# Four PSUM banks for the transposed expert rows, and 16-bit integer lookups in the expert choice

## What is computed

```
q = (ht @ w_query).reshape(T, 8, 2, 128)
s = einsum('thpd,hpnd->thpn', q, sub_keys)          # 8 heads, 2 halves, 128 keys
top_s, top_i = top_k(s, 16)
cand_s = top_s[:, :, 0, :, None] + top_s[:, :, 1, None, :]     # 16 x 16 sums a head
cand_i = top_i[:, :, 0, :, None] * 128 + top_i[:, :, 1, None, :]
fin_s, pos = top_k(cand_s, 16)
fin_i = take_along_axis(cand_i, pos)                # 128 experts a token
gate = softmax(fin_s)
out = sum over the 128: gate * gelu(expert_u[fin_i] . x) * expert_v[fin_i]
```

## Time and profile before

| | us |
|---|---|
| median of 3 runs (3353.91 to 3363.41) | 3357.28 |
| the profiled execution's own time | 3359.51 |
| its span in the trace | 3357.8 |
| busy: TensorE matmul / weight load | 3265.7 / 2872.9 |
| busy: VectorE / ScalarE / GpSimd | 2549.1 / 900.3 / 801.7 |
| `peer_topk`, 887.9 to 1511.5 | 623.6 |
| `peer_gates`, 1511.5 to 2267.2 | 755.7 |
| `peer_down`, 2267.2 to the end | 1090.6 |

### The profile page before, as it was taken

The page is one execution under the profiler, slowest core; times in us unless marked ns, Lnnn a source line. Parts: engine busy times, 40 slices in busy tenths (PEclk is TensorE's granted clock), DMA queues, the critical chain, the costliest instruction groups (busy, mean ns, idle before and its releaser), DMA issues. The chain is left out here.

```text
span 3357.8 us, 46048 instructions
## 1 busy us (share of the span) xinstructions
PE 3265.7 (97%) x17796; PEld 2872.9 (86%) x17796; DVE 2549.1 (76%) x5349; ACT 900.3 (27%) x1310; POOL 801.7 (24%) x625
## 2 busy tenths in 40 slices
PE   8999989899999999999999999999999999999998
PEld 7867755499999999999999999997888888888887
DVE  6611244322499999999989898876999999999996
ACT  4210301111122222224444444432222222222222
POOL 0000000000001100104333333342444444444440
PEclk9999989899999999999999999999999999999999
DMA  3010021311144444448889788889898898988883
GB/s 99 14 40 27 13 88 63 119 57 38 46 133 145 144 141 141 134 137 291 304 308 325 279 324 308 308 320 359 312 318 306 314 314 314 312 318 314 316 309 135
DMA packets 332962, 695.58 MB, mean 207 GB/s; under 512 B 34332, under 2 KB 194936, under 8 KB 326584
## 3 DMA queue, kind: packets, MB, share of 16 engines
q1 hardware_dynamic: 248600, 386.28, 33.0%
q0 software_dynamic: 84144, 306.35, 26.7%
HBM read 580.10 MB, written 110.64 MB: 206 GB/s over the span
## 5 line engine op out<-in xcount | busy, mean ns | idle before, releaser
L1782 ACT ACTIVATE up_a<-up_pa 128x384 f32<-128x384 f32 x256 | 126.0, 492 | 830.8 <-PE up_pa L1767 820.9
L1806 POOL DMA_INDIRECT lead<-in_peer_v_dram,idx x174 | 259.6, 1492 | 352.9 <-DVE acc_s L1825 326.7
L2478 DVE TENSOR_TENSOR acc<-pd_po,acc 128x512 f32<-128x512 f32 x384 | 264.6, 689 | 93.3 <-PE pd_po L2537 90.7
L1806 POOL DMA_INDIRECT gr_row<-in_peer_u_dram,idx x192 | 229.9, 1197 | 368.2 <-DVE raw L1815 341.3
L1815 DVE CUSTOM_DVE_ANT_0 gr_row<-gr_row,xs 128x1024 f32<-128x1024 f32 x192 | 232.1, 1223 | 2.1 <-DMA gr_row<-in_peer_u_dram,idx 2.0
L1806 POOL DMA_INDIRECT dr_row<-in_peer_v_dram,idx x114 | 171.1, 1501 | 215.1 <-DVE acc_s L1825 211.7
L1825 DVE SCALAR_TENSOR_TENSOR acc_s<-lead,gate,acc_s 128x1024 f32<-128x1024 f32 x174 | 222.3, 1278 | 0.0
L2264 DVE TENSOR_SCALAR pg_hot_i<-pg_iota,sel_t 128x128 f32<-128x128 f32 x768 | 214.2, 359 | 0.0
L511 PE MATMUL fr_a<-pj_w,h_t 128*128 128x256 f32 (+1 forms) x864 | 200.3, 394 | 0.9 <-PEq L186 0.9
L2299 PE MATMUL pg_pw<-pg_hot_i,pg_hot_j 128*128 128x128 f32 x1536 | 200.5, 276 | 0.1
L511 PEld LDWEIGHTS fr_a<-pj_w,h_t 128*128 128x128 f32 (+1 forms) x864 | 171.0, 227 | 29.7 <-issue 8.4
(11 more groups left out here) (469 smaller groups left out, 7899.0 us busy)
## 6 DMA issues: line engine op xcount, KB each, us to landing
lead<-in_peer_u_dram SPq DMA_DIRECT2D x128, 512.0 KB, 4.9
room<-in_peer_v_dram SPq DMA_DIRECT2D x128, 512.0 KB, 4.5
act_d<-up_a SPq DMA_DIRECT2D x256, 192.0 KB, 3.5
room<-w_d SPq DMA_DIRECT2D x64, 768.0 KB, 6.6
room<-act_d SPq DMA_DIRECT2D x64, 768.0 KB, 9.2
w_d<-room SPq DMA_DIRECT2D x24, 1024.0 KB, 10.6
w_d<-pg_wb SPq DMA_DIRECT2D x24, 1024.0 KB, 9.0
pj_w<-in_w_in_dram SPq DMA_DIRECT2D x8, 1024.0 KB, 5.7
```

Source lines behind the costliest of these rows:

```text
L1782: self.nc.scalar.activation(self.a_sb[c][:], self.pa[c][:, 0:WB], ACT.Gelu_apprx_tanh).then_inc(self.a_act, 1)
L1806: pool.indirect_dma_start(self.buf[i % self.n], None, self.table, bass.IndirectOffsetOnAxis(ap=self.idx[:, col:col + 1], axis=0)).then_inc ...
L2478: nc.vector.tensor_tensor(out, po[(OUTS * g + o) % NPO][:], out, ALU.add).then_inc(o_added, 1)
```

## The change

The transposed pieces get four PSUM banks, two for even and two for odd blocks, and `turn(n, half)` waits for the low part of block n-2 in place of n-1. In the choice, indices and positions are cast to 16-bit whole numbers; the row 0 to 15 becomes a table `places` of 16x128 16-bit numbers, made by the same GpSimd instruction; the masks `met` are 16-bit and lie one after the other in the room of `w2`, laid out with the 16 places outermost and the heads innermost; and the sum over 16 is done by halving: 8 with 8, 4 with 4, 2 with 2, and a last addition that writes float32. `pos2` moves into `w2`. Two `beside` points at the sums stay, in slightly other places. In `build`, the gap that brings the addresses to a multiple of 256 bytes moves ahead of `Up`'s identity, which leaves what follows where it was.

```
     def place_turns(self, ctx, nc):
-        self.pt = [... psum_tensor(f"up_pt{b}", [P, W4], F32)) for b in range(2)]
+        self.pt = [... psum_tensor(f"up_pt{b}", [P, W4], F32)) for b in range(4)]
+
+    def turn_bank(self, n, half):
+        return self.pt[2 * (n % 2) + half]
...
     def turn(self, pe, n, half):
         if half == 0:
             pe.wait_ge(self.u_in[n % 2], 16 * (n // 2 + 1))
-        if n >= 1:
-            pe.wait_ge(self.ut_lo, 2 * (n - 1) + half + 1)
+        if n >= 2:
+            pe.wait_ge(self.ut_lo, 2 * (n - 2) + half + 1)
...            (high and low read turn_bank(n, half) too)
-        idxf = sb("idxf", [P, PH, 2, TOPK])
+        ids_h = sb("ids_h", [P, 2, TOPK, PH], U16)
...
-        pos2 = sb("pos2", [P, 2, PH, TOPK], U32)
-        posf = sb("posf", [P, 2, PH, TOPK])
-        iota = sb("iota", [P, TOPK])
+        pos2 = w2[:]...bitcast(U32)[:, 0:2 * NSEL]...
+        pos_h = sb("pos_h", [P, 2, TOPK, PH], U16)
+        places = sb("places", [P, TOPK, PH * TOPK], U16)
+        met = w2[:]...bitcast(U16).rearrange("p (i m s) -> p i m s", i=2, m=TOPK)
...
-            nc.gpsimd.iota(iota[:], [[1, TOPK]], ...)
+            nc.gpsimd.iota(places[:], [[1, TOPK], [0, PH * TOPK]], ...)
...
-                did(v.tensor_copy(idxf[:], ids[:]))
+                did(v.tensor_copy(ids_h[:].rearrange("p i m h -> p h i m"), ids[:]))
...
-                did(v.tensor_copy(posf[:], pos2[:]))
+                did(v.tensor_copy(pos_h[:].rearrange("p i k h -> p i h k"), pos2[:]))
...
                 for i in range(2):
-                    did(v.tensor_tensor(oh[i], iota (broadcast), posf[:, i] (broadcast), ALU.is_equal))
+                    did(v.tensor_tensor(met[:, i], places[:], pos_h[:, i] (broadcast), ALU.is_equal))
                     beside(22 + i)
                 settle()
                 for i in range(2):
-                    did(v.tensor_tensor(o4, o4, idxf[:, :, i, :] (broadcast), ALU.mult))
+                    did(v.tensor_tensor(m4, m4, ids_h[:, i] (broadcast), ALU.mult))
                     beside(24 + i)
                 settle()
...
-                for i in range(2):
-                    did(v.tensor_reduce(res[:, i]..., oh[i], AX.X, ALU.add))
-                    beside(26 + i)
+                for n in (8, 4, 2):
+                    did(v.tensor_tensor(met[:, :, 0:n], met[:, :, 0:n], met[:, :, n:2 * n], ALU.add))
+                    if n == 8:
+                        beside(26)
+                    settle()
+                did(v.tensor_tensor(res[:, 0:2]..., met[:, :, 0]..., met[:, :, 1]..., ALU.add))
+                beside(27)
```

More of the change, by code:

```diff
@@ L1730, in place_turns @@
     def place_turns(self, ctx, nc):
-        self.pt = [ctx.enter_context(nc.psum_tensor(f"up_pt{b}", [P, W4], F32)) for b in range(2)]
+        self.pt = [ctx.enter_context(nc.psum_tensor(f"up_pt{b}", [P, W4], F32)) for b in range(4)]
+    def turn_bank(self, n, half):
+        return self.pt[2 * (n % 2) + half]
     def load(self, sp, n):
@@ L1752, in turn @@
             pe.wait_ge(self.u_in[n % 2], 16 * (n // 2 + 1))
-        if n >= 1:
-            pe.wait_ge(self.ut_lo, 2 * (n - 1) + half + 1)
+        if n >= 2:
+            pe.wait_ge(self.ut_lo, 2 * (n - 2) + half + 1)
         for k in range(4):
             c = (4 * half + k) * P
-            mm = self.nc.tensor.transpose(self.pt[half][:, k * P:(k + 1) * P], self.u_sb[n % 2][:, c:c + P], self.ident[:])
+            mm = self.nc.tensor.transpose(self.turn_bank(n, half)[:, k * P:(k + 1) * P], self.u_sb[n % 2][:, c:c + P], self.ident[:])
         mm.then_inc(self.turned, 1)
@@ L1775, in high @@
         self.nc.scalar.activation(self.ut[n % self.NB][0][:, 4 * half:4 * half + 4, :],
-                                  self.pt[half][:].rearrange("p (k s) -> p k s", k=4), ACT.Copy).then_inc(self.ut_hi, 1)
+                                  self.turn_bank(n, half)[:].rearrange("p (k s) -> p k s", k=4), ACT.Copy).then_inc(self.ut_hi, 1)
     def gelu(self, act, n, c):
@@ L1786, in low @@
         dve.wait_ge(self.ut_hi, 2 * n + half + 1)
-        self.nc.vector.tensor_tensor(self.ut[n % self.NB][1][:, k, :], self.pt[half][:].rearrange("p (k s) -> p k s", k=4),
+        self.nc.vector.tensor_tensor(self.ut[n % self.NB][1][:, k, :], self.turn_bank(n, half)[:].rearrange("p (k s) -> p k s", k=4),
                                      self.ut[n % self.NB][0][:, k, :].bitcast(F32), ALU.subtract).then_inc(self.ut_lo, 1)
@@ L1858, in peer_topk @@
         ids = sb("ids", [P, PH, 2, TOPK], U32)
-        idxf = sb("idxf", [P, PH, 2, TOPK])
+        ids_h = sb("ids_h", [P, 2, TOPK, PH], U16)
         fin = sb("fin", [P, PH, TOPK])
         pos = sb("pos", [P, PH, TOPK], U32)
-        pos2 = sb("pos2", [P, 2, PH, TOPK], U32)
-        posf = sb("posf", [P, 2, PH, TOPK])
-        iota = sb("iota", [P, TOPK])
+        pos2 = w2[:].rearrange("p u k -> p (u k)").bitcast(U32)[:, 0:2 * NSEL].rearrange("p (i h k) -> p i h k", i=2, h=PH)
+        pos_h = sb("pos_h", [P, 2, TOPK, PH], U16)
+        places = sb("places", [P, TOPK, PH * TOPK], U16)
+        met = w2[:].rearrange("p u k -> p (u k)").bitcast(U16).rearrange("p (i m s) -> p i m s", i=2, m=TOPK)
         res = sb("res", [P, 3, PH, TOPK])
@@ L1883, in _ @@
         def _(pool):
-            nc.gpsimd.iota(iota[:], [[1, TOPK]], base=0, channel_multiplier=0,
+            nc.gpsimd.iota(places[:], [[1, TOPK], [0, PH * TOPK]], base=0, channel_multiplier=0,
                            allow_small_or_imprecise_dtypes=True).then_inc(shaped, 1)
@@ L1985, in _ @@
                 cand, cand2 = (x.rearrange("p u k -> p (u k)").rearrange("p (h k) -> p h k", k=K2) for x in (w1, w2[:]))
-                oh = [x.rearrange("p u k -> p (u k)").rearrange("p (s m) -> p s m", m=TOPK) for x in (w1, w2[:])]
                 units = [(a, i) for a in range(PH) for i in range(2)]
@@ L2049, in _ @@
                 for i in range(2):
-                    did(v.tensor_tensor(oh[i], iota[:].unsqueeze(1).broadcast_to([P, PH * TOPK, TOPK]),
-                                        posf[:, i].rearrange("p h k -> p (h k)").unsqueeze(2)
-                                        .broadcast_to([P, PH * TOPK, TOPK]), ALU.is_equal))
+                    did(v.tensor_tensor(met[:, i], places[:], pos_h[:, i].rearrange("p k h -> p (k h)").unsqueeze(1)
+                                        .broadcast_to([P, TOPK, PH * TOPK]), ALU.is_equal))
                     beside(22 + i)
@@ L2055, in _ @@
                 for i in range(2):
-                    o4 = oh[i].rearrange("p (h k) m -> p h k m", k=TOPK)
-                    did(v.tensor_tensor(o4, o4, idxf[:, :, i, :].unsqueeze(2).broadcast_to([P, PH, TOPK, TOPK]), ALU.mult))
+                    m4 = met[:, i].rearrange("p m (k h) -> p m k h", h=PH)
+                    did(v.tensor_tensor(m4, m4, ids_h[:, i].unsqueeze(2).broadcast_to([P, TOPK, TOPK, PH]), ALU.mult))
                     beside(24 + i)
@@ L2061, in _ @@
                     dve.wait_ge(turned, q - 3)
-                for i in range(2):
-                    did(v.tensor_reduce(res[:, i].rearrange("p h k -> p (h k)"), oh[i], AX.X, ALU.add))
-                    beside(26 + i)
+                for n in (8, 4, 2):
[3 more added lines that the diff above has]
+                    settle()
+                did(v.tensor_tensor(res[:, 0:2].rearrange("p i h k -> p i k h"),
+                                    met[:, :, 0].rearrange("p i (k h) -> p i k h", h=PH),
+                                    met[:, :, 1].rearrange("p i (k h) -> p i k h", h=PH), ALU.add))
+                beside(27)
                 dve.wait_ge(ex_out, q + 1)
@@ L2614, in build @@
             raw = ctx.enter_context(nc.sbuf_tensor("raw", [P, COLS], F32))
+            to_boundary(ctx, nc, "left", 64, boundary=256)
             up = Up(ctx, nc, lead, u_d, act_d)
             turns = ExitStack()
-            to_boundary(ctx, nc, "left", 64, boundary=256)
             with ExitStack() as c1:
```

## The result

The changed kernel takes 3331.02 us (median of 6, 3327.56 to 3333.29) against 3357.18 of before (median of 6): 26.2 us less, ratio 0.992, 95% interval 0.9907 to 0.9933. The forecast was 3330.

A forecast was written before the change was run, and what follows sets the result against it. TensorE bounds, stalled in the choice stage by VectorE's late low part: 617.97 us less 590.6 leaves 27.4, less 0.3 at the start, so -27 from the profiled 3359.5 gives 3332.5; 2.2 above the median, hence 3330, range 3322 to 3350.

The forecast's parts named there:

- the 27.4 us: Choice stage, first product to last transposes: 617.97 us less TensorE's own 590.6; 15.6 stalls, the rest mostly low clock.
- Part 1: Four banks: the stall inside `turn` goes, then VectorE sets the pace; alone 1.2 us a choice, about 10 us in eight.
- what is late next: After the `turn` stall goes: `up(n, 0)`, which needs both low parts of block n, ready 2.5 us early at first.
- The pace of 66.8: Choice stage: VectorE with the float32 lookup needs 66.8 us a choice, more than TensorE's 64.75.
- the corner: Choice stage: the VectorE load that decides, TensorE's 64.75 us a choice; staying under it takes a saving of 2.1 us.
- the first rival: Lookup: 16-bit operations run at the float32 rate, VectorE needs 67.0 us a choice and sets the pace; 3350, chance 0.12.
- Part 2: 16-bit lookup in the choice: VectorE saves 5.9 us a choice and needs 60.9; alone it gives nearly nothing.
- The lower bound of the 16-bit cost: Lookup: two elements a step, 1.22 us for 2048 numbers, 7.3 us start to start for the new operations.
- The two casts: Lookup: keep 256 elements, 0.29 us; writing every eighth 16-bit number adds 0 to 0.3 us each, hidden below 64.75.
- Part 3: Stage start and rest: larger table takes 1.95 us, first product +0.3 us later (0 to +2); moved gap costs nothing.
- the slow layout: Lookup: masks in rows of eight short numbers make VectorE need 75.8 us a choice; +62 us, 3419, chance 0.03.
- a gain given back: Behind the choice stage: gate-stage waits or a new stall before `up(n, 0)` return half of the 27; 3344, chance 0.05.

## Why the prediction was right

**What bounds the stage.** The two readings held: one stall in eight of the nine choices through a late low part, and under it a VectorE that needs more than TensorE. TensorE alone was put at 590.6 us from the first product to the last transposes; the changed kernel takes 591.3, from 885.43 to 1476.71. The split of the 27.4 us held too: TensorE's busy time fell by 11.2 us (604.89 to 593.71) with the same matmuls, against the 11.8 left to the low clock.

**Part 1.** The wait left the `turn`, and "what is late next" was `up(n, 0)`, as the run with the banks alone shows. Its size was undersold: 16 us in place of 10. The pace of 66.8 was right to 0.3 us, but I let it run through all eight choices where the reserve covers the first two, which go at TensorE's own 64.8. This did not enter the forecast, since with the 16-bit lookup VectorE is under the corner; it does enter the price of the first rival, which was worked out in the same way. The 66.5 us a choice of the run with the banks alone gave 3342; the rival's 67.0 would give some 3345 by the same account (six choices at 0.5 us more), and not 3350.

**Part 2.** The lower bound of the 16-bit cost was the true one: 1214 ns against 1.22 us. The Trainium skill (VectorE: DVE Perf Modes, The perf-mode tier table), which the prediction named, gives 1224 ns for `tensor_tensor` on 2048 bf16 numbers. The runs agree with 1211 to 1216 ns, here for 16-bit whole numbers and for inputs that repeat. That this half gives nothing alone was right within 1 us (3357.49 against 3358.23 of before in the same round).

**The mis-sized terms** both lay below the corner, where VectorE's work is hidden. The two casts cost 0.46 us more each, over my 0 to 0.3, and the last addition 0.19 more. So VectorE needs 61.7 us a choice and not 60.9. That leaves 3.1 us a choice, so none of it reached the time. The added operations show the limit: 2.3 us more are free and 4.6 are not.

**Part 3.** The table's iota took 1888 ns (1.95 forecast). VectorE's first low part starts 2.0 us behind the first transpose in place of 1.4, the 0.6 forecast. The first product starts 3.32 us behind the first transpose (882.11 to 885.43), 3.12 before (887.90 to 891.02): +0.2, forecast +0.3. The barrier's gap stayed at 2.02. The gate stage gave 0.

**The rivals.** The float32 rate, the slow layout and a gain given back are each excluded by a row above: 1214 ns; 61.7 us a choice, far from 68.0; 755.77 us in the gate stage.

## What to carry to other kernels

When an engine A waits briefly for an engine B once in each round, compare two numbers before choosing a cure: the need of each engine in a round, and how late the one instruction is in its place. A buffer or a better place takes the lateness away, but in the long run a round stays as long as the slower engine needs: 66.5 us here with the float32 lookup, in place of 68.0. Less work on B cured nothing here while B waited for A to fill the next buffer. Work that is hidden stays free only to the corner: the first 2.3 us added to a choice cost 0.8 us in all, the next 3.7 and the next 18.7 (by the profiled stages 0.1, 7.8 and 17.4).

## What the runs showed that I had not expected

The low clock does not follow every pause. Before, pauses of 1.95 us inside a `turn`, with four transposes on each side, brought TensorE to 1.2 GHz for a time behind six of eight; with the 16-bit lookup and two banks it was again six of eight. With three operations added, six pauses of 1.88 to 1.91 us ahead of a product brought none in the stage, two of them here:

```profile
1139.90 1.68 PE L1770 MATMUL up_pa<-h_dh,up_ut0h 128*128 128x384 f32 x8 [1.91 <-DVE up_ut0l L1790]
...
1208.08 1.68 PE L1770 MATMUL up_pa<-h_dh,up_ut1h 128*128 128x384 f32 x8 [1.89 <-DVE up_ut1l L1790]
```

Nor did the shorter pauses inside a `turn` with the low part moved and the float32 lookup (1.58 us at most). Busy time around one such pause, first before, then with three added:

```profile
1211.00:1217.00 6.00, 5.24 (x23) 5.25 (x24) 5.79 (x9) 0.60 (x1) 0.00 (x0) 0.72 0.50 177
```

```profile
1139.00:1145.00 6.00, 5.10 (x33) 5.07 (x33) 5.82 (x11) 3.01 (x5) 0.00 (x0) 1.00 0.23 89
```

The granted clock is 0.72 in the one and 1.00 in the other, with less busy time in the second. So nearly the same idle time cost some 3.6 us in one place (1.94 and the 1.65 of the slow matmuls) and 1.9 in the other. The pauses differ in their length by some 0.05 us, in the work around them and in the moment at which they come; what decides was not tried, and two of the eight pauses inside a `turn` had no low clock behind them either.
